# Low halves of the up weights made on GpSimd in place of VectorE, in a one-core encoder step

## The reference, cut to what matters

```
h  = x @ w_in                                      # q | k | v | u, 512 columns each
a  = stick-breaking attention(q, k, v)             # 8 heads x 64
p  = pooled means of u, mapped per group
x1 = LayerNorm(ALPHA * x + concat[a, p] @ w_out)
y  = LayerNorm(ALPHA * x1 + (silu(x1 @ w_gate) * (x1 @ w_up)) @ w_down)
```

## Time and profile before

| | |
|---|---|
| median of three runs | 3116.81 us |
| the profiled execution: time, span | 3123.18 us, 3121.5 us |
| TensorE busy (matmul) | 2739.5 us, 88% of the span |
| VectorE busy | 1719.5 us, 55% |
| ScalarE busy | 1022.8 us, 33% |
| GpSimd busy | 676.4 us, 22% |
| granted TensorE clock, mean | 0.938 |

### The profile page before, as it was taken

How to read it: one execution, slowest core, us unless ns; L and a number is a source line. 1 busy time by engine, 2 the same in 40 slices (tenths; PEclk the granted TensorE clock), 3 DMA queues, 4 the chain that set the end, 5 groups by cost and what they waited for, 6 DMA issues and landing times.

```text
span 3121.5 us, 38457 instructions
## 1 busy us (share of the span) xinstructions
PE 2739.5 (88%) x14298; PEld 2338.4 (75%) x14298; DVE 1719.5 (55%) x2206; ACT 1022.8 (33%) x1758; POOL 676.4 (22%) x823
## 2 busy tenths in 40 slices
PE   4999995479987898978999998889989898899996
PEld 3999994367766787766777786667777697899995
DVE  3122265536862245758776457687876436744444
ACT  3111133315541122444544123455544212222221
POOL 4000033122321002315221004263332003300003
PEclk7999996679997799999999999999999999999998
DMA  7344416525445623424432524344432522322221
GB/s 288 101 138 142 138 69 167 171 58 137 127 116 132 209 75 93 113 86 141 112 105 81 203 75 115 99 144 114 117 109 77 184 88 68 102 82 83 87 81 56
DMA packets 385802, 365.39 MB, mean 117 GB/s; under 512 B 21623, under 2 KB 317935, under 8 KB 382558
## 3 DMA queue, kind: packets, MB, share of 16 engines
q1 hardware_dynamic: 383198, 354.70, 38.3%
q0 software_dynamic: 2432, 8.39, 0.8%
HBM read 294.94 MB, written 68.09 MB: 116 GB/s over the span
## 4 chain that ended last, share of the span: by engine, by line
PE 59%; DVE 11%; issue 4%; DMA 4%; SPq 3%; ACT 2%; POOL 1%; POOLq 0%; DVEq 0%; ACTq 0%
PE bank L1333 27%; PE bank L1349 12%; PE bank L1298 6%; PE bank L1226 5%; PE bank L1272 4%; PE bank L1244 4%; DVE left L1554 3%; DVE gw_lo L1615 2%; DMA dw_lo_raw<-in_w_down_dram 1%; SPq L1120 1%; DVE aT L1561 1%; DVE acc L1582 1%; SPq L1097 1%; PE bank L1264 1%; DMA k_st<-kT_scratch 1%
## 5 line engine op out<-in xcount | busy, mean ns | idle before, releaser
L1333 PE MATMUL bank<-x1T,gw_hi 128*128 128x512 f32 (+1 forms) x3520 | 954.2, 360 | 41.3 <-DVE hT_lo_raw L1627 32.4
L1333 PEld LDWEIGHTS bank<-x1T,gw_hi 128*128 128x128 f32 x3520 | 627.9, 193 | 135.7 <-issue 44.3
L1333 PE MATMUL bank<-x1T,gw_lo 128*128 128x512 f32 (+1 forms) x1760 | 630.4, 358 | 0.0
L1777 POOL TENSOR_TENSOR beta<-beta,left 128x512 f32<-128x512 f32 (+2 forms) x326 | 338.3, 1038 | 822.9 <-DVE left L1554 822.5
L1554 DVE TENSOR_TENSOR_SCAN left<-bank,left,zero_t 128x512 f32<-128x512 f32 (+2 forms) x326 | 361.9, 1111 | 33.7 <-ACT bank L1397 25.9
L1333 PEld LDWEIGHTS bank<-x1T,gw_lo 128*128 128x128 f32 x1760 | 338.4, 192 | 50.2
L1655 DVE TENSOR_TENSOR acc<-bank,acc 128x512 f32<-128x512 f32 x320 | 218.8, 687 | 283.0 <-PE bank L1349 282.5
L1226 PE MATMUL bank<-k_st,q_st 128*128 128x512 f32 (+3 forms) x688 | 235.0, 413 | 150.6 <-DVE left L1554 80.0
L555 PE MATMUL bank<-xT,whi 128*128 128x416 f32 x1280 | 348.9, 354 | 5.1 <-DVE wlo L657 4.2
L1396 ACT ACTIVATE beta<-bank 128x512 f32<-128x512 f32 (+2 forms) x326 | 173.5, 532 | 539.9 <-PE bank L1226 539.3
L1349 PE MATMUL bank<-dw_hi,hT_hi 128*128 128x512 f32 x748 | 307.2, 411 | 29.6 <-DVE hT_lo L1643 14.9
(11 more groups left out here) (133 smaller groups left out, 3542.1 us busy)
## 6 DMA issues: line engine op xcount, KB each, us to landing
gw_lo_raw<-in_w_gate_dram SPq DMA_DIRECT2D x88, 512.0 KB, 3.9
gw_lo_raw<-in_w_up_dram SPq DMA_DIRECT2D x88, 512.0 KB, 3.9
dw_lo_raw<-in_w_down_dram SPq DMA_DIRECT2D x88, 512.0 KB, 4.5
k_st<-kT_scratch SPq DMA_DIRECT2D x160, 256.0 KB, 4.4
v_st<-v_scratch SPq DMA_DIRECT2D x80, 256.0 KB, 3.5
wo_raw<-in_w_out_dram SPq DMA_DIRECT2D x16, 1024.0 KB, 6.0
mixT<-mixT_scratch SPq DMA_DIRECT2D x8, 2048.0 KB, 13.2
qT_scratch<-parts SPq DMA_DIRECT2D x8, 1040.0 KB, 5.6
```

Source lines behind the costliest of these rows:

```text
L1333: m = pe.matmul(gu_bank(g, n)[:, 0:w], gw[L % 4][a][:, k, :], x1T[x][:, k, first:first + w], start=k == 0 and s == 0, stop=k == KD - 1 and ...
L1777: pool.tensor_tensor(x[:, 0:w], x[:, 0:w], left[n % RL][:, 1:w + 1], ALU.mult).then_inc(a_done, 1)
```

## The change

The 88 low halves of up tiles are computed by GpSimd instead of VectorE. The subtraction, its operands and its place in the list of slots are the same. TensorE waits on a semaphore of its own for each kind (`g_lo` for gate tiles, `u_lo` for up tiles). VectorE keeps the 88 gate tiles.

```diff
-    g_hi, g_lo, d_hi, d_lo = (sem(n) for n in ("g_hi", "g_lo", "d_hi", "d_lo"))
+    g_hi, g_lo, u_lo, d_hi, d_lo = (sem(n) for n in ("g_hi", "g_lo", "u_lo", "d_hi", "d_lo"))
@@ TensorE, gate
-                    pe.wait_ge(g_lo, L + 1)
+                    pe.wait_ge((g_lo, u_lo)[g], L // 2 + 1)
@@ VectorE
-            for L in range(4):
+            for L in (0, 2):
                 gate_lo(L)
...
-                        if i == 0 and pair:
-                            gate_lo(4 * pair + 1)
...
-                            if d == 3:
-                                gate_lo(4 * pair + 3)
...
-                        if i == 3 and p == 0 and pair:
-                            gate_lo(4 * pair + 3)
@@ GpSimd
+            def up_lo(L):
+                pool.wait_ge(g_hi, L + 1)
+                pool.tensor_tensor(gw[L % 4][1][:], gw[L % 4][2][:], r32(gw[L % 4][0][:]), ALU.subtract).then_inc(u_lo, 1)
...
+            for L in (1, 3):
+                up_lo(L)
...
+                        if i == 0 and pair:
+                            up_lo(4 * pair + 1)
...
+                            if d == 3:
+                                up_lo(4 * pair + 3)
...
+                        if i == 3 and p == 0 and pair:
+                            up_lo(4 * pair + 3)
                         if i >= 2 and p == 0 and b:
                             affine(ln_index(2, b - 1), i - 2)
```

More of the change, by code:

```diff
@@ L1816, in _ @@
                 for p in range(PAIRS):
+                    pair = PAIRS * b + p
                     for i in range(4):
                         background(next(slot))
+                        if i == 0 and pair:
+                            up_lo(4 * pair + 1)
                     if p:
```

## The result

The changed kernel takes 3099.57 us (median of four runs, 3098.38 to 3108.81) against 3117.59 us (3115.76 to 3120.5) for the kernel before beside it: 18 us faster. The ratio is 0.9948, with a 95% interval of 0.9927 to 0.9969. Repeated with the last experiments it took 3101.70 us, ratio 0.9953 (0.9939 to 0.9966). The forecast was 3104 us, 13 us faster. The profiled execution took 3108.81 us, with a span of 3107.2 us: 14.3 us less than the span before.

A forecast was written before the change was run, and what follows sets the result against it. TensorE, 88% busy, was taken as the bound, its idle time in attention stretches spent waiting for scans in VectorE's queue. 23 - 2 - 2 - 2 - 4 = 13 us of gain, from 3116.81 to 3104 us; range 3093 to 3120.

The forecast's parts named there:

- What is removed: VectorE loses 88 up-tile subtractions; half of the 46.8 us that L1615 holds on the chain, 23 us, is won.
- short waits: At four places like L = 87, TensorE's wait is shorter than the subtraction, so 2 us of gain are lost.
- What is added: 88 subtractions of 2.5 us, 220 us, on GpSimd; its mean 3.0 us pause before products covers them in ordinary pairs.
- the new wait for ScalarE: GpSimd's wait for ScalarE's high half is seldom the last to end; otherwise the same pause covers it, costing nothing.
- L = 91: At block 2's first pair, the tile stands among GpSimd's LayerNorm operations and delays an awaited product; 2 us charged.
- L = 135: At the last block's first pair, the tile may come a microsecond late, before a 3.38 us wait that swallows it.
- The lock: GpSimd's up tiles hold up VectorE operations in attention stretches: 19 us of VectorE's time, 4 us on the path.
- the LayerNorm places: At L = 47 and 81, up tiles met a LayerNorm on VectorE; their neighbours still do, so 2 us come off.
- The first rival: Once the subtraction is gone, sigmoids or an `acc` addition are late instead; 3.5 us gain, 3113 us; chance 0.22.
- The second: GpSimd's tiles meet VectorE's operations regularly at each of 54 tiles; 6 us slower, 3123 us; chance 0.10.
- The third: Products come 0.25 us late for transposes at 54 tiles in ordinary pairs; 13.5 us lost, 3117 us; chance 0.07.
- The fourth: Fewer meetings in the other direction also speed up GpSimd; gain above 20 us, 3094 us; chance 0.05.

The follow-up runs named there:

- the removal alone: Against the kernel before: nobody computes the up tiles' low halves, TensorE multiplies the high half again instead; 3085.08 us, ratio 0.9896.
- the complement: Against the changed kernel: only the 48 up tiles without attention beside them, plus L = 47 and 91, on GpSimd, 40 on VectorE; 3123.20 us, ratio 1.0019.
- six operations per pair: Against the changed kernel: only attention stretches' gate and up tiles on GpSimd, plus the down weights' low halves of 18 pairs; 3087.00 us, ratio 0.9901.

## Why the prediction was right

The time, its direction and the mechanism came out: 18 us measured, 13 forecast. The forecast time lies as near as it does partly by luck: the sum was made of two terms that were both too small, 21 us of gain against 32 and 8 us of cost against 14 to 17, and they made up for each other.

- **What is removed**, 23 us less 2 for short waits: measured by the removal alone, 32 us. Half of the chain's 46.8 us was a fair reading of the waiting: TensorE's idle time fell by 18.4 us between the traces. What the sum lacked is the speed of TensorE's own work, which was busy for 19.7 us less. At L = 4 to 16 the rows show how: no wait of 1.89 us, and no slower clock behind it. How much of the 19.7 us comes in this way and how much is chance in the clock was not separated: the kernel before took 3112.09 us in an execution with a mean granted clock of 0.943, and 3120.74 us in one with 0.937.
- **What is added**: 2.40 us per tile against 2.5 taken. GpSimd's mean pause covers it in attention stretches: TensorE still waits for a product only once. That the new wait for ScalarE is seldom the last was wrong: from 690 to 2440 us GpSimd waited for `gw_hi` 33 times, 390.8 us. The one product that TensorE waited for was not behind such a wait: at L = 91 the subtraction follows the operation before it without a pause.

```profile
POOL gw_lo L1806 <- ACT gw_hi L1436: 390.8, 33, 45.7
```

- **L = 91**, 2 us: TensorE's wait grew by 3.5 us, and 0.6 to 3.1 us of progress went, of which some 1.5 us go without this tile too.
- **L = 135** nearly on time: right, TensorE waited 0.2 us there, the only wait for a tile of GpSimd's in the whole run. In the pair of the earlier trace rows little came back: from L = 124 to 140 the two traces of the changed kernel won 1.1 and 3.2 us, the removal alone 4.2.
- **The lock**, 4 us, with 2 more for the LayerNorm places: a term that was sized wrong. Making the tiles on GpSimd costs 14 to 17 us in all, against 8 in the sum. VectorE's lengthening was about right: I had 19 us, and its busy time is 1633.6 us against 1614.0 with the tiles removed, 19.6 us for the same 2118 instructions. The fifth of it that I put on the path seems to have been too little. I spread chance meetings over attention stretches (and counted 27 pairs there, where scans run beside 23). But costly meetings stand at fixed places outside attention: `wo_lo` with L = 27, which I had not counted among the vulnerable operations, and `o_lo` with L = 119. Each is followed by a wait of TensorE, the first also by a slower clock. In the trace of the 48 tiles, 2.2, 4.7 and 2.6 us go between L = 24 and 28, 88 and 92, and 116 and 124; that these three places are the whole of its 5 us was not shown. Nor did the runs part the 14 to 17 us into lock, queue and clock.
- **The first rival**, a smaller gain since something else is late: no; TensorE got back more than the up tiles' share of the chain. **The second**, slower through the lock: only the complement is slower, and with meetings at a few places, not at each tile. **The third**, GpSimd's queue: no, not even at six operations per pair. **The fourth**, a gain above 20 us since GpSimd gets faster too: in part. With the tiles removed, its same 823 instructions took 656.0 us in place of 676.4, and in the changed kernel the 88 subtractions took 225.2 us while its busy time rose by 203. The gain stayed at 18 us all the same.

## What to carry to other kernels

Before moving work to an idle engine, ask of each copy of it what waits behind it in its present queue. Only the copies that stand ahead of an awaited operation are worth moving: here 40 of 88 carried the gain. Where two engines lock each other, look at the places where the same two long operations meet in every run, and keep those few copies where they are. A chain of waits tells what an operation holds up. It does not tell how much faster TensorE's own work gets when its waits are gone; compare TensorE's busy time for the same number of matmuls as well.

## What the runs showed of the hardware

- A VectorE operation with two SBUF inputs that starts while GpSimd reads takes its own time plus about what is left of GpSimd's operation: `wo_lo` took 4.48 us with 2.33 us left and 3.29 with 1.14 left, against 2.29 alone. Beside GpSimd's memsets, which only write, it took 2.28. The Trainium skill states both (SBUF — State Buffer, "Who interferes with whom"), and these rows agree.
- Having one SBUF tile as input did not protect an operation: VectorE's LayerNorm operation (L1582) took 0.81 us alone and up to 2.89 in a meeting.
- A wait of TensorE of 3.08 us was followed by 3.7 us at a granted clock of 0.54, the lower of its two levels for most of it, with matmuls 0.43 us apart; before it and from 1098.4 us on the clock was 1.00, with matmuls 0.23 us apart where they ran at 512 columns. (1 - 0.54) x 3.7 = 1.7 us came on top of a wait that was 2.2 us longer than the 0.88 us of before. Together they make 3.9 us, about the 3.7 lost there. Behind the 0.88 us wait of the kernel before (window 1101 to 1105 us) the clock was 1.00. A wait of 1.89 us in the kernel before was followed by 3.4 us at 0.50, one of 1.30 us at the same place of the changed kernel by none.
- GpSimd needs 2.40 us for a subtraction of 128 x 1024 that takes VectorE 1.22.
